# Query weight units that come in among the expert rows: each loaded in two transfers over parts of the partitions

## The reference

```python
q = (xt @ w_q).reshape(n_tok, PEER_HEADS, 2, PEER_DKEY // 2)      # w_q is 2048 x 2048
s = jnp.einsum('nhcd,hckd->nhck', q, sub_keys)
s1, i1 = lax.top_k(s[:, :, 0], PEER_TOPK)
s2, i2 = lax.top_k(s[:, :, 1], PEER_TOPK)
...
ub = u_tab[eb]                                                    # 8 heads x 16 experts for each token
h = jax.nn.gelu(jnp.einsum('td,thed->the', xb, ub), approximate=False)
vb = v_tab[eb]
return jnp.einsum('the,thed->td', gb * h, vb)
```

## Time and profile before

| | |
|---|---|
| median of 3 runs | 1745.6 us (1744.86 to 1746.58) |
| span of the profiled execution | 1744.5 us |
| busy: PE, PEld, DVE | 1503.3, 876.6, 1198.7 us |
| busy: ACT, POOL | 311.4, 330.5 us |
| moved by DMA | 636.98 MB, 365 GB/s over the span |

### The profile page before, as it was taken

How to read it: one execution, slowest core, us unless ns; L and a number is a source line. 1 busy time by engine, 2 the same in 40 slices (tenths; PEclk the granted TensorE clock), 3 DMA queues, 4 the chain that set the end, 5 groups by cost and what they waited for, 6 DMA issues and landing times. The chain is left out here.

```text
span 1744.5 us, 15291 instructions
## 1 busy us (share of the span) xinstructions
PE 1503.3 (86%) x5516; PEld 876.6 (50%) x5516; DVE 1198.7 (69%) x2105; ACT 311.4 (18%) x611; POOL 330.5 (19%) x294
## 2 busy tenths in 40 slices
PE   9999999999998989999778788777777877777874
PEld 8999899888654545455333333323233323333321
DVE  4699999667656565657576666767575756666657
ACT  5443455633110101010100101010101101010100
POOL 0101101101121211313221222212212222221221
PEclk9999999999999999999999999999999999999998
DMA  6665544664999999999999999999999999999995
GB/s 239 204 230 191 193 146 146 246 258 159 430 426 427 428 427 428 427 428 429 429 428 428 428 428 428 428 428 428 429 428 428 426 427 425 415 421 426 427 427 211
DMA packets 54313, 636.98 MB, mean 365 GB/s; under 512 B 6354, under 2 KB 7026, under 8 KB 10098
## 3 DMA queue, kind: packets, MB, share of 16 engines
q0 software_dynamic: 39616, 549.47, 74.6%
q1 hardware_dynamic: 13972, 86.66, 13.5%
q10 hardware_dynamic: 672, 0.21, 0.1%
HBM read 632.12 MB, written 4.19 MB: 365 GB/s over the span
## 5 line engine op out<-in xcount | busy, mean ns | idle before, releaser
L716 PE MATMUL psum<-uv_row,scratch 128*128 128x512 f32 x2032 | 963.7, 622 | 223.2 <-DVE scratch L1433 216.1
L1425 DVE CUSTOM_DVE_ANT_0 uv_row<-uv_row,x 128x2048 f32<-128x2048 f32 x256 | 586.6, 2291 | 402.7 <-DMA uv_row<-in_uv_tab,eid 402.6
L716 PEld LDWEIGHTS psum<-uv_row,scratch 128*128 128x128 f32 x2032 | 385.9, 197 | 759.9 <-issue 402.4
L382 POOL DMA_INDIRECT uv_row<-in_uv_tab,eid x252 | 284.9, 1131 | 994.9 <-PE psum L716 954.7
L1011 ACT ACTIVATE gel<-dots 128x1 f32<-128x1 f32 x256 | 51.9, 203 | 1130.0 <-DVE dots L1425 1130.0
L412 PE MATMUL psum<-xT_hi,w_hi 128*128 128x256 f32 x640 | 183.0, 286 | 2.1 <-DVE w_lo L1088 1.6
L413 PE MATMUL psum<-xT_lo,w_hi 128*128 128x256 f32 x640 | 181.1, 283 | 0.0
L414 PE MATMUL psum<-xT_hi,w_lo 128*128 128x256 f32 x640 | 181.0, 283 | 0.0
L1088 DVE TENSOR_TENSOR w_lo<-w_raw,w_hi 128x2048 fp32r<-128x2048 f32 x62 | 141.7, 2287 | 27.9 <-ACT w_hi L812 27.0
L812 ACT ACTIVATE w_hi<-w_raw 128x2048 fp32r<-128x2048 f32 x62 | 118.8, 1916 | 84.2 <-DMA w_raw<-in_w_stream 84.2
L1433 DVE TENSOR_SCALAR scratch<-ident,gel,gate 128x128 f32<-128x128 f32 x256 | 101.8, 398 | 45.7 <-ACT gel L1011 41.3
(11 more groups left out here) (199 smaller groups left out, 928.4 us busy)
## 6 DMA issues: line engine op xcount, KB each, us to landing
w_raw<-in_w_stream SPq DMA_DIRECT2D x63, 1024.0 KB, 4.8
wq_first<-in_w_stream SPq DMA_DIRECT2D x8, 1024.0 KB, 11.7
wq_third<-in_w_stream SPq DMA_DIRECT2D x4, 1024.0 KB, 11.7
uv_row<-in_uv_tab,eid POOLq DMA_INDIRECT x252, 22.2
xT_raw<-in_xT SPq DMA_DIRECT2D x4, 512.0 KB, 6.8
turned_rows<-dist_row POOLq DMA_DIRECT2D x1, 2048.0 KB, 14.5
bias<-turned_rows POOLq DMA_DIRECT2D x1, 2048.0 KB, 15.0
wq_first<-in_w_stream POOLq DMA_DIRECT2D x1, 2048.0 KB, 8.1
```

The source lines that it names most:

```text
L382: pool.indirect_dma_start(dst, None, tab, bass.IndirectOffsetOnAxis(ap=ids, axis=0)).then_inc(land, 16)
L716: last = pe.matmul(bank(tile, n), diag[k], row[k][:, D + n * 512:D + (n + 1) * 512], start=False, stop=True, skip_group_check=True)
L1425: dve.tensor_tensor_reduce(row[k][:, 0:D], row[k][:, 0:D], x1[:, s // SLOTS, :], 1.0, 0.0, ALU.mult, ALU.add, dots[:, s:s + 1]).then_inc(d ...
```

## The change

SP issues each of the twelve unit loads as two transfers, over the partitions below and above a cut. The cut is 64 for the first eight units (`u` 4 to 11) and 120 (`MOST`) for the last four (`u` 12 to 15, from `UNEVEN = 12`). Both add 16 to the same semaphore, and PE waits for 32 a use where it waited for 16.

```diff
+MOST = 15 * P // 16
+UNEVEN = 2 * PH - 4
...
-                sp.dma_start(wq_unit[(u - 4) % UNITS], w_stream[U_WQ + u]).then_inc(wq_in[(u - 4) % UNITS], 16)
+                k, cut = (u - 4) % UNITS, MOST if u >= UNEVEN else P // 2
+                for part in (slice(0, cut), slice(cut, P)):
+                    sp.dma_start(wq_unit[k][part], w_stream[U_WQ + u][part]).then_inc(wq_in[k], 16)
...
-                    pe.wait_ge(wq_in[k], uses * 16)
+                    pe.wait_ge(wq_in[k], uses * 32)
```

## The result

The changed kernel takes 1803.6 us (median of 5 runs, 1802.3 to 1809.7) against 1745.6 us before. The ratio is 1.0335, with an interval of 1.0323 to 1.0346, so +58 us. The forecast was 1768 us with a range from 1735 to 1776 us; the direction was right and the size was not.

A forecast was written before the change was run, and what follows sets the result against it. The prediction took the 16 DMA engines to bound the kernel. Even splits, 17.2 us, plus cuts at 120, 4.9 us, made 22.1 us on 1745.6, given as 1768 us, range 1735 to 1776 us.

The forecast's parts named there:

- What bounds the kernel: Row stream: the 16 DMA engines set the pace at 4.90 us a row; DVE needs 2.29, PE 2.5 us.
- More issues: SP's queue: twelve more transfers at 0.33 us each, 4 us spread over 300 us, taken as nothing.
- landing later: Unit loads: each has about 60 us and uses 11.7, 18.7 at most, so later landing costs nothing.
- The shape: Split unit loads: engines writing half the SBUF share half its ways in; 17.2 us for seven even splits.
- a unit occupies the engines for up to twice its 2.45 us: Evenly split units beside the rows: +2.45 us a unit on all engines, 7 x 2.45 = 17.2 us.
- The upper bound of 3.0 us: Evenly split units: highest price a unit, from the trace's 2.24 times slower `turned_rows` transfer at 191 GB/s.
- The price of 120 and 8: Last four units: between nothing and 2.45 us each, the middle 1.2 taken, 4.9 us in all.
- The faster rival: Tail of one late DMA engine: the cut at 120 spares it 9.8 us, giving 1736 us; chance 24%.
- No difference: Split units: engines work past each other and the late one isn't spared, 1745.6 or 1746.9 us; chance 15%.
- both hold: Split units: ways shared and late engine spared, about 1758 us; counted in the forecast's case of 61%.
- What would show it: Windows 466 to 760 us: share 1.0 below 428 GB/s, 9.4 MB missing; no new PE wait, tail stays.

The follow-up runs named there:

- e3: Changed kernel, but each unit split by columns into two transfers over all 128 partitions: 1747.6 us, ratio 0.9998 to the kernel before.
- e1: Changed kernel, but all twelve units cut at partition 64: 1798.5 us, ratio 1.0303 to the kernel before.
- e7: Changed kernel, but the first eight units split by columns and only the last four cut at 120: 1769.5 us, ratio 1.0144 to the kernel before.
- e2: Changed kernel, but all twelve units cut at partition 120: 1811.0 us, ratio 1.0358 to the kernel before.
- e6: Changed kernel, but all twelve units cut at partition 112: 1793.7 us, ratio 1.0281 to the kernel before.

## Why the prediction was right and where it was wrong

*What bounds the kernel* held: the loss is DMA time between 442 and 880 us, one to one, and nothing else moved. One figure in it was misread. PE needs not 4 x 0.622 = 2.5 us a row: L716 has 2032 matmuls, eight a row, and 963.7 us of busy time for 254 rows are 3.8 us a row. That is still less than 4.90, so the bound stays, with less room.

*More issues, and landing later, taken as nothing*: right. PE has no wait behind a unit, and e3 with the same number of transfers is at 0.9998.

*The shape.* The mechanism named was right in kind, as far as it can be seen: the engines hold one another up, at a full busy share. That it is a way in which they share stays argued. Alone, the even cut did run at half rate, as its price supposed. These are windows of the changed kernel while the first unit loads before the rows, 422 to 426 us; the kernel before shows 397 and 377 GB/s in its windows of 422 to 424 and 424 to 426 us, for the same loads unsplit:

```profile
420.00:422.00 2.00, 2.00 (x10) 1.68 (x9) 1.86 (x9) 0.00 (x0) 0.00 (x0) 1.00 1.07 393
422.00:424.00 2.00, 1.09 (x5) 0.56 (x3) 1.90 (x9) 0.00 (x0) 0.00 (x0) 1.00 0.96 188
424.00:426.00 2.00, 1.78 (x8) 1.63 (x9) 1.90 (x10) 0.00 (x0) 0.00 (x0) 1.00 0.93 205
```

The step that failed is the term "a unit occupies the engines for up to twice its 2.45 us", +2.45 us a unit and 17.2 us for seven. It measured 4.7 a unit (e1), so a unit occupies them for 2.9 times its 2.45 us. The longer time of the unit's own packets was counted, and for the even cuts it was even too high: 15.6 us over eleven units, 1.4 each. What was left out is the other party: the rows' packets beside a unit take some 1.6 times as long too (995 ns on average for those over 700 in e1), and each is twice the size. That was 36.0 us of 51.6 in e1. The upper bound of 3.0 us had the same fault, since it too came from a transfer that ran nearly by itself, and so the range ended at 1776 us.

*The price of 120 and 8*, "the middle, 1.2": 5.8 us (e7). The reason given, that nearly all ways stay in use, is refuted as a measure of the price by e2 and e6. The other half of that sentence, that the packets may be dealt in another order and meet, was nearer: the transfer is slow even without the rows (578 ns a packet with the cut at 120, against 309). Nothing bounded its price at 2.45. The middle of a range was taken for want of a row, and it was off by a factor of five.

*The faster rival*: half true. One engine has less to do, and runs ahead; it is not the late one, and the tail stayed at 7 us in the changed kernel, e2 and e7. *No difference* and *both hold*: refuted.

*What would show it*: the share of 1.0 with fewer GB/s came as written, with 438 us x (428 - 370) GB/s = 25 MB missing instead of 9.4 MB.

## What to carry to other kernels

Where the DMA engines are the bound, read share and GB/s together: here a share of 1.0 at a lower rate was packets that took 1.5 to 1.7 times as long, and the price fell mostly on the traffic beside the transfer that was changed, 2 to 4 us for each 1 us of its own. Bound such a price by what it can do to the others' packets, not by the transfer's own time. If a tile must be split, split it by columns, or over every second or fourth partition; do not cut it into a lower and an upper block. To try a shape cheaply, time its packets with nothing beside them: in these runs every part that was slow beside the rows was slow alone, and none that was free.

## What the runs showed of the hardware that I had not expected

- A load cut at 112 or at 120 is about as bad as one cut at 64: 4.3 and 5.8 us a unit of 1 MB against 4.7.
- The middle, partitions 32 to 95, costs nothing, and the two quarters around it cost as much for each MB as an even cut.
- Every second and every fourth partition cost nothing (0.9999 and 1.0001), every eighth 63.5 us.
- With 120 partitions one of the 16 DMA engines runs 10 us ahead of the others at row 40, while another remains some 7 us behind all to the end, as in the kernel before, the changed one and e7.
